# One completion count a chunk in place of four for the scaled keys of a chunked mLSTM

## The reference, cut to what matters

```python
def step(carry, inp):
    C, n, m = carry
    ...
    s = jnp.einsum('bhtd,bhsd->bhts', q_, k_) * dexp
    num = jnp.einsum('bhts,bhsd->bhtd', s, v_) + inter_w[..., None] * jnp.einsum('bhtd,bhde->bhte', q_, C)
    den = jnp.sum(s, axis=-1) + inter_w * jnp.einsum('bhtd,bhd->bht', q_, n)
    h = num / jnp.maximum(jnp.abs(den), jnp.exp(-m_t))[..., None]
    ...
    C_new = decay[..., None, None] * C + jnp.einsum('bhs,bhsd,bhse->bhde', ws, k_, v_)
    n_new = decay[..., None] * n + jnp.einsum('bhs,bhsd->bhd', ws, k_)
    return (C_new, n_new, m_new), h
```

## Time and profile before

| what | value |
|---|---|
| median of three runs | 2774.16 us (2771.98 to 2777.65) |
| the profiled execution | 2774.16 us |
| its span, first to last instruction | 2772.2 us |
| outside the span | 1.96 us |
| mean granted TensorE clock | 0.969 |
| the mLSTM's chunks in the span | 1496 to 1616 us |

### The profile page before, as it was taken

The page is one execution under the profiler, slowest core; times in us unless marked ns, Lnnn a source line. Parts: engine busy times, 40 slices in busy tenths (PEclk is TensorE's granted clock), DMA queues, the critical chain, the costliest instruction groups (busy, mean ns, idle before and its releaser), DMA issues. The chain is left out here.

```text
span 2772.2 us, 30843 instructions
## 1 busy us (share of the span) xinstructions
PE 2558.4 (92%) x12104; PEld 2077.1 (75%) x12104; DVE 1320.1 (48%) x1716; ACT 1183.8 (43%) x1709; POOL 636.2 (23%) x520
## 2 busy tenths in 40 slices
PE   7999988889999999999998979999985999999992
PEld 6888866667787888878887868785774888888881
DVE  5530217773304112135433643105126888888885
ACT  4212227773341222123322622235224787777772
POOL 2312302313221122233211542354101111111100
PEclk9999999999999999999998999999987999999996
DMA  5433135523311031132225632441444999999995
GB/s 178 150 120 107 46 88 132 146 69 122 114 46 46 31 134 39 72 100 99 76 76 160 197 107 76 141 156 61 149 160 167 373 384 379 381 377 374 374 367 204
DMA packets 168691, 455.78 MB, mean 164 GB/s; under 512 B 17921, under 2 KB 85665, under 8 KB 155873
## 3 DMA queue, kind: packets, MB, share of 16 engines
q1 hardware_dynamic: 117856, 384.98, 38.4%
q10 hardware_dynamic: 37760, 41.17, 4.3%
q0 software_dynamic: 12928, 27.63, 2.9%
HBM read 389.23 MB, written 82.31 MB: 170 GB/s over the span
## 5 line engine op out<-in xcount | busy, mean ns | idle before, releaser
L2672 DVE TENSOR_TENSOR ex_w_lo<-ex_w,ex_w_hi 128x2048 fp32r<-128x2048 f32 x198 | 448.0, 2290 | 82.4 <-ACT ex_w_hi L2617 80.6
L2617 ACT ACTIVATE ex_w_hi<-ex_w 128x2048 fp32r<-128x2048 f32 x198 | 378.9, 1914 | 51.7 <-PEq L2218 26.4
L219 POOL TENSOR_TENSOR p_w_lo<-w_raw,p_w_hi 128x512 fp32r<-128x512 f32 (+1 forms) x154 | 203.3, 1352 | 633.0 <-ACT p_w_hi L239 606.9
L219 POOL TENSOR_TENSOR p_w_lo_rest<-w_raw,p_w_hi_rest 128x512 fp32r<-128x512 f32 x94 | 125.4, 1369 | 254.6 <-ACT p_w_hi_rest L239 254.5
L264 PE MATMUL o_ps<-o_w_hi,o_m_hi 128*128 128x512 f32 x384 | 153.7, 400 | 11.0 <-DVE split_cols L1175 11.0
L266 PE MATMUL o_ps<-o_w_hi,split_cols 128*128 128x512 f32 x384 | 152.3, 397 | 0.0
L265 PE MATMUL o_ps<-o_w_lo,o_m_hi 128*128 128x512 f32 x384 | 151.9, 396 | 0.0
L264 PE MATMUL p_ps<-p_w_hi,hT_hi 128*128 128x512 f32 (+1 forms) x320 | 121.2, 379 | 0.0
L2484 POOL DMA_INDIRECT ex_x<-xn_rows,slot_token x33 | 36.0, 1090 | 360.8 <-PE ex_px L2531 325.9
L266 PE MATMUL p_ps<-p_w_hi,hT_lo 128*128 128x512 f32 (+1 forms) x320 | 118.7, 371 | 0.0
L265 PE MATMUL p_ps<-p_w_lo,hT_hi 128*128 128x512 f32 (+1 forms) x320 | 118.4, 370 | 0.0
(11 more groups left out here) (475 smaller groups left out, 6449.9 us busy)
## 6 DMA issues: line engine op xcount, KB each, us to landing
ex_w<-w SPq DMA_DIRECT2D x99, 2048.0 KB, 14.0
w_raw<-w_in SPq DMA_DIRECT2D x42, 1024.0 KB, 5.2
x_rows<-o_x SPq DMA_DIRECT2D x24, 512.0 KB, 2.6
att_k<-k_columns SPq DMA_DIRECT2D x46, 256.0 KB, 7.3
w_raw<-w_out SPq DMA_DIRECT2D x8, 1024.0 KB, 9.9
qk_columns<-qk_y ACTq DMA_DIRECT2D x16, 512.0 KB, 2.6
o_x<-x_rows SPq DMA_DIRECT2D x16, 512.0 KB, 4.1
w_raw<-w_xkv SPq DMA_DIRECT2D x8, 1024.0 KB, 6.0
```

Of the source, the lines that this page charges most:

```text
L219: emit(self.lo(n)[:, 0:w], self.half(n // (KC // 2), w)[:, n % (KC // 2), :], self.hi(n)[:, 0:w].bitcast(F32), ALU.subtract).then_inc(self ...
L2617: nc.scalar.activation(w_hi[:, n % RING, :], raw_half(n), ACT.Copy).then_inc(hi_done, 1)
L2672: nc.vector.tensor_tensor(w_lo[:, n % RING, :], raw_half(n), w_hi[:, n % RING, :].bitcast(F32), ALU.subtract).then_inc(down_lo if m == "w2 ...
```

## The change

Before, each of the four key instructions of a chunk (L1907) counts `kn_ready` up by one, and PE's update of head h waits for the count u + 1, which is its own head's key instruction. After, only the fourth instruction of a chunk counts, by one, and PE's updates of all four heads wait for t + 1, which is the fourth instruction. `turn_mixed` waits for the same moment as before, the last key instruction of its chunk, by the new count.

```diff
@@ turn_mixed (PE)
                     pe.wait_ge(m_ready, t + 1)
-                    pe.wait_ge(kn_ready, MH * keys)
+                    pe.wait_ge(kn_ready, keys)
@@ the heads of a chunk (PE)
                         ins.then_inc(n_done, 1)
-                        pe.wait_ge(kn_ready, u + 1)
+                        pe.wait_ge(kn_ready, t + 1)
                         if u >= 1:
                             pe.wait_ge(c_ready, u)
@@ keys (ACT)
                     for h in range(MH):
-                        nc.scalar.activation(kn[:, h * MD:(h + 1) * MD], p_t[:, h * MD:(h + 1) * MD],
-                                             ACT.Copy, scale=cols[:, t, C_WS, h:h + 1]).then_inc(kn_ready, 1)
+                        ins = nc.scalar.activation(kn[:, h * MD:(h + 1) * MD], p_t[:, h * MD:(h + 1) * MD],
+                                                   ACT.Copy, scale=cols[:, t, C_WS, h:h + 1])
+                    ins.then_inc(kn_ready, 1)
```

## The result

The changed kernel takes 2790.66 us, the median of five runs (2785.8 to 2793.62), against 2774.16 for the kernel before beside it (2771.98 to 2778.33). The medians lie 16.5 us apart; the ratio over the executions is 1.0054, with a 95% interval of 1.0041 to 1.0067, which is 15 us slower, between 11.4 and 18.6. The forecast was 2788.8 us, 14.6 slower.

A forecast was written before the change was run, and what follows sets the result against it. The prediction took a gapless loop of ACT, PE and DVE, 15.79 us a chunk, as the bound. Six chunks losing 2.44 us (1.09 wait, 1.35 block) add 14.6 to 2774.16, giving 2788.8 us, range 2780 to 2795.

The forecast's parts named there:

- The loop: mLSTM chunks: a gapless chain through ACT, PE and DVE from one chunk's key instructions to the next's, 15.79 us a round.
- The keys' wait: Chunks 1 to 6: PE's update of head 0 waits for the fourth key instruction and starts 1.09 us later.
- The block: Chunks 1 to 6: POOL's L1719 starts 0.13 us ahead and keeps DVE's L1817 out, 1.35 us more a chunk.
- The sum: Six chunks lose 2.44 us each, 14.6 us in all, giving 2788.8 us.
- The counts: ACT: three key instructions a chunk no longer count up; taken as nothing, at most a gain of 1 us.
- Chunks 0 and 7: Chunk 0 has its keys early, chunk 7's update of head 0 starts 0.52 us later but hidden: nothing lost.
- The cover: Chunk 7: DVE's last mixing waits 1.89 us for the second branch, hiding 0.52 us; without it, 0.5 us lost.
- DVE is first: Rival: L1817 starts ahead of L1719 and takes 0.69 us; 2.2 us slower in all, 2776.3 us; chance 0.09.
- Only the keys' wait counts: Rival: POOL slows L1817 by a fixed amount, so it stays 1.42 us; 6.5 us slower, 2780.7 us; chance 0.08.
- PE's clock falls: Rival: PE drops to 1.2 GHz in longer gaps; some 80 us more over six chunks, about 2855; chance 0.02.

The follow-up runs named there:

- e1: Kernel before with its four counts a chunk, but PE's updates of all heads wait for the fourth key instruction; ratio 1.0054, round 18.22 us.
- e2: Kernel before, but PE's update of head 0 waits for the third key instruction; ratio 1.0009, round 16.15 us.
- e3: Kernel before, but PE's update of head 0 waits for the second key instruction; ratio 0.9998, round 15.80 us.
- e5: Changed kernel, but L1817 reads the causal mask from PSUM and PE's numerator of head 3 waits for the weighting; ratio 1.0023, round 16.51 us.
- e7: Changed kernel, but POOL starts L1719 only when the next chunk's weighting is done; ratio 1.0017, round 16.51 us.
- e4: Kernel before, but in chunks 0 and 7 alone PE's updates wait for all four key instructions; ratio 0.9992, round 15.78 us.
- e9: Kernel before with head 0 waiting for the third key instruction and the next carry spread behind head 2's numerator; ratio 1.0000, round 15.93 us.
- e11: Kernel before with the causal mask in PSUM and the next carry spread behind head 2's numerator; ratio 0.9984, round 15.20 us.
- e10: Changed kernel with the causal mask in PSUM and the next carry spread behind head 2's numerator; ratio 1.0005, round 16.29 us.

## Why the prediction was right

*The loop.* The key instruction of head 0 was a link of it: one edit of PE's wait in e1 gave the whole loss.

*The keys' wait, 1.09 us.* It measured 1.60 - 0.51 = 1.09.

*The block, 1.35 us more.* L1817 took 2.75 and ended 0.55 behind L1719, which was back at 2.35. The order of starts held in all six chunks, with 0.14 to 0.15 us between them where 0.13 was forecast. The steps of e2 and e3 and the two cures of e5 and e7 show that it is this block and not the wait as such. Seven kernels of this document leave both operands of L1817 in SBUF and let POOL run freely (before, changed, e1 to e4, e9). In all 42 chunks of them that have POOL beside it, L1817 started 0.13 to 2.22 us behind a POOL instruction and ended 0.54 to 0.56 us behind its end. The Trainium skill (SBUF — State Buffer, Who interferes with whom) has this as a rule: whoever issues first has the shared pair for the whole instruction, and the other blocks. The traces agree in every one of these chunks. That the lead of POOL would stay on its side at 0.13 us was read from two pairs with leads of 0.02 and 0.12; it was argued, not luck, but it was narrow, and 0.36 us less of a wait (e2) gave the other order.

*The sum.* 6 x 2.44 = 14.6 was forecast. The five rounds from chunk 1 to chunk 6 grew by 2.42 each, and the stretch from there to chunk 7 by 2.71, together 14.84. The 0.29 by which the last is larger are the key transposes, which ran in part at the lower clock in this execution (1.38 us, not 1.09).

*The counts.* Taken at nothing: e1 and the changed kernel differ by 0.01 us in length.

*Chunks 0 and 7.* Taken at nothing, and e4 lost nothing. In the changed kernel the last mixing on DVE waited 0.40 us for the landing of the second branch, where it had been 1.89; it started 11.92 us behind the first keys of chunk 7, against 12.01. The cover held, with less to spare. The lower clock of this execution had made PE late there too, so the 0.52 us of the forecast have no row that shows them alone.

*The rivals.* "DVE is first" has its mechanism confirmed by e7, where it was made so, but its price was too low: the forecast gave 0.36 us a round, e7 has 0.72. "Only the keys' wait counts" would give 16.88 in the changed kernel and 16.51 in e2; neither came. "PE's clock falls" did not happen inside the rounds, where the window has 1.00. It fell between chunk 6 and chunk 7, for 0.29 us. The forecast excluded it by a row that says less than I took from it: 3.5 us of idle time at full clock in one execution does not exclude the lower level in another. Its price was summed low too: six chunks with 15.4 us more each are some 92 us, not 80.

*What the prediction missed* without harm to its sum is how near the second path was. I wrote that behind L1817 DVE has no room, which is so, but not that PE's numerator of head 2 comes only 0.36 us ahead of DVE's need. With the fourth key instruction L1817's own delay of 2.44 covers that path; with the smaller delays of e2, e5 and e7 it sets the round. That the sum came to no harm by it was luck: the forecast had not weighed that path.

## What to carry to other kernels

A wait moved by a microsecond costs what it meets, not what it is: here 0.36 us more of it were free, the next 0.36 cost 0.36, and the last 0.36 cost 2.06, because an instruction fell behind the start of a long one on another engine. When a wait is merged or moved, look in the timeline for every instruction with two SBUF inputs behind it on DVE, and for POOL's next start: with tenths of a microsecond between them the same step can cost nearly six times as much. One operand in PSUM kept such an instruction out of the contest in every chunk here (0.68 us each time). Then take the next path in turn, here PE's own order, since each cure was paid only down to the second path.

## What the runs showed of the hardware that was not expected

PE sat idle for 3.4 to 3.5 us ahead of chunk 7's key transposes in all fourteen profiles. The granted clock was 1.00 in the next stretch of five of them and averaged 0.50 to 0.68 in nine, and both outcomes stand behind 3.37 us of idle time (e11 and e10) and behind 3.50 (the kernel before and e4). A wait shown ahead of a weight load overstated the loss: 0.31 us of it were worth 0.14 us of a round, in two pairs of kernels. When DVE was already waiting as POOL's L1717 ended, DVE got in ahead of L1719, though L1719 stood next in POOL's queue: this is so in the kernel before and in e3, where L1717's end and L1719's start lie only 0.08 us apart.
